# Opening of a hybrid decoder block on one core: modulation and state-space products by channel halves, transfers issued from the SyncE queue

## What is computed

```
c_act = silu(c)
mod = c_act @ w_ada + b_ada                  # six rows of 1024: sh1, sc1, g1, sh2, sc2, g2
h = rmsnorm(x, norm1_g) * (1.0 + sc1) + sh1
z = h @ w_in                                 # 1024 x 3584: conv input and gate, ssm input, two gates
u_conv, u_ssm, gl_conv, gl_ssm = split(z)
y_conv = conformer_conv(u_conv, ...)         # 31-tap causal depthwise convolution, layernorm, silu, projection
y_ssm = s5_mixer(u_ssm, ...)                 # 32 groups of 16 channels, 64 complex states, gelu, GLU
merged = sigmoid(gl_conv) * y_conv + sigmoid(gl_ssm) * y_ssm
x = x + g1 * (merged @ w_out)
```

## Time and profile before

| | us |
|---|---|
| median of 3 runs | 2529.43 |
| lowest, highest | 2527.99, 2530.13 |
| the profiled execution | 2530.5 |
| its span | 2528.7 |
| PE busy in the span | 2489.5 |
| DVE, ACT, POOL busy | 1651.0, 875.9, 1724.7 |
| mean granted TensorE clock, share of full | 0.994 |

### The profile page before, as it was taken

One profiled execution on the slowest core, in us unless ns is written; L12 is line 12 of the kernel. 1 busy time (PEld: TensorE's weight loads), 2 busy tenths in 40 slices (PEclk: granted clock), 3 DMA queues, 4 the chain that ended last, 5 costly groups with the idle time before them and its releaser, 6 DMA issues.

```text
span 2528.7 us, 31370 instructions
## 1 busy us (share of the span) xinstructions
PE 2489.5 (98%) x11419; PEld 2050.1 (81%) x11419; DVE 1651.0 (65%) x2038; ACT 875.9 (35%) x1379; POOL 1724.7 (68%) x1182
## 2 busy tenths in 40 slices
PE   7999999999999999999999999999999999999998
PEld 3888788888888888888788888878878888888886
DVE  5899639945596648946833334575654336899798
ACT  4322421153012421146533345443222334445444
POOL 2777777677866777675787767797778764445444
PEclk9999999999999999999999999999999999999999
DMA  8676357553666347472332232324566327465533
GB/s 278 201 200 217 117 161 222 155 167 119 212 173 191 123 159 224 136 225 90 123 96 76 79 112 93 109 86 148 175 190 193 103 88 252 144 226 183 197 99 117
DMA packets 426161, 395.66 MB, mean 156 GB/s; under 512 B 92232, under 2 KB 330520, under 8 KB 424472
## 3 DMA queue, kind: packets, MB, share of 16 engines
q1 hardware_dynamic: 324688, 319.93, 40.6%
q10 hardware_dynamic: 101320, 73.72, 9.5%
HBM read 317.88 MB, written 67.24 MB: 152 GB/s over the span
## 4 chain that ended last, share of the span: by engine, by line
PE 84%; DVE 6%; DMA 3%; issue 2%; ACT 2%; POOL 1%; ACTq 1%; SPq 0%; POOLq 0%; DVEq 0%
PE bank L1926 19%; PE bank L1928 19%; PE bank L1927 19%; PE bank L2171 5%; PE bank L2172 5%; PE bank L2173 5%; DMA row_pair<-in_w_ffn_out 3%; PE bank L2085 2%; PE bank L2087 2%; PE bank L2086 2%; PE bank L2006 1%; PE bank L2005 1%; DVE bank L1027 1%; PE bank L1991 1%; DMA ada<-in_w_ada 1%
## 5 line engine op out<-in xcount | busy, mean ns | idle before, releaser
L2258 POOL TENSOR_TENSOR w_lo<-raw,w_hi 128x1024 fp32r<-128x1024 f32 x192 | 479.6, 2498 | 36.7 <-ACT w_hi L1383 12.5
L2254 POOL CAST w_hi<-raw 128x1024 fp32r<-128x1024 f32 x186 | 199.5, 1073 | 346.2 <-PE bank L1928 272.0
L1926 PE MATMUL bank<-h_hi,w_hi 128*128 128x512 f32 x896 | 352.3, 393 | 1.0 <-ACT wm L1322 0.9
L1928 PE MATMUL bank<-h_hi,w_lo 128*128 128x512 f32 x896 | 349.9, 390 | 0.0
L1927 PE MATMUL bank<-h_lo,w_hi 128*128 128x512 f32 x896 | 349.5, 390 | 0.0
L839 DVE SCALAR_TENSOR_TENSOR bank<-uc,cwt,bank 128x512 f32<-128x512 f32 x464 | 323.2, 751 | 6.2
L2281 POOL TENSOR_TENSOR fw_lo<-fsum,fw_hi 128x512 fp32r<-128x512 f32 x176 | 237.8, 1355 | 71.3 <-ACT fw_hi L1615 71.2
L1926 PE MATMUL bank<-xc_hi_T,fw_hi 128*128 128x512 f32 x704 | 276.4, 393 | 5.8 <-DVE tr L1032 4.6
L1927 PE MATMUL bank<-xc_lo_T,fw_hi 128*128 128x512 f32 x704 | 274.8, 390 | 0.0
L1928 PE MATMUL bank<-xc_hi_T,fw_lo 128*128 128x512 f32 x704 | 274.6, 390 | 0.0
L2308 POOL TENSOR_TENSOR ow_lo<-raw,ow_hi 128x512 fp32r<-128x512 f32 x116 | 161.4, 1392 | 163.3 <-ACT ow_hi L1662 163.3
(11 more groups left out here) (341 smaller groups left out, 5246.4 us busy)
## 6 DMA issues: line engine op xcount, KB each, us to landing
raw<-in_w_in SPq DMA_DIRECT2D x112, 512.0 KB, 3.9
raw<-in_w_ffn_in SPq DMA_DIRECT2D x66, 512.0 KB, 6.0
hid_scratch<-tr SPq DMA_DIRECT2D x88, 256.0 KB, 3.2
raw<-tsum_scratch SPq DMA_DIRECT2D x66, 256.0 KB, 3.2
g2b<-in_w_ada SPq DMA_DIRECT2D x64, 256.0 KB, 3.9
ssm_m<-vk_scratch SPq DMA_DIRECT2D x32, 512.0 KB, 5.0
raw<-in_ssm_glu SPq DMA_DIRECT2D x32, 512.0 KB, 3.8
raw<-in_w_out SPq DMA_DIRECT2D x32, 512.0 KB, 3.6
```

Of the source, the lines that this page charges most:

```text
L1926: t.matmul(dst, wh, xh, start=first, stop=False)
L1928: return t.matmul(dst, wl, xh, start=False, stop=last)
L2254: g.tensor_copy(hi[:], src[:]).then_inc(hi_done, 1)
L2258: g.tensor_tensor(lo[:], src[:], hi[:].bitcast(F32), ALU.subtract).then_inc(split_done, 1)
```

## The change

The change rewrites the opening of block 0.

- **Halves.** The modulation is made in two halves by output channel (kinds sh1 and sc1 together). PE's rows of half 0 go into `bank[2]`, of half 1 into `bank[7]`. Each half has its own sums, `modrow`, turn and scale (`modulation_sums`, `modulation_turn` and `modulation_half`). PE keeps slabs 1, 3 and 5; DVE takes 0, 2, 4, 6 and 7.
- **Products.** The first four weight chunks are no longer one per output tile. Chunk (pair, half) holds 256 output columns, which are two ssm tiles, for 4 of the 8 channel tiles. PE runs pair 0 on channels 0 to 3 (step "A0"), then pair 1 on 0 to 3 ("A1"), then pair 0 on 4 to 7 and pair 1 on 4 to 7 (`ssm_rest`). us0 and us1 are thus done together, and so are us2 and us3.
- **Order.** PE puts the turns, the sums of the second half, the transposes of h4 to h7 and those of `nat_b` between these products; `nat_w` (v2) comes after hl7 and ahead of the products of channel tile 7. DVE puts the first angles and the mean and root of x's norm ahead of slab 2, and slab 4's four steps between hl0 and hl3. ACT applies h0 to h3 ahead of the exponentials and sines.
- **Transfers.** c comes by itself in `nat_c`, issued first by ACT, and is turned on PE into `bank[6]`, from where ACT takes silu; a Silu on one column ("pre") goes ahead of it. ACT issues that, two tiles of x and the step sizes. SP issues the rest: slab 0, two tiles of x, slab 1, the vectors, the poles, slabs 2 and 3, two weight chunks, slabs 4 to 7, `nat_b`, the next two chunks, and then the small parameters.

The diff, cut to its core:

```diff
-    FIRST_CHUNKS = [ssm_chunks + sum(conv_chunks, [])]
+    FIRST_CHUNKS = [[("us", pair_, half) for half in range(2) for pair_ in range(KS // 2)] + sum(conv_chunks, [])]
...
-        pe_pro = ["v1", "ada1", "v0", "ada3", "ada5", "ada6", "ada7", "sums", "mt"] + h_steps[0:4] + ["bx"] + h_steps[4:] + ["v2"]
+        pe_pro = ["vc", "ada1", "v1", "v0", "ada3", "sums0", "h0", "h1", "mt0", "h2", "h3", "A0", "ada5", "h4", "sums1",
+                  "mt1", "h5", "bx", "A1", "h6", "h7", "v2"]
...
-        act_pro = ["cs", "dt"] + norm_act + [f"nx{i}" for i in R(TT)] + ["ej", "m8", "sj", "cj"] + h_act
+        act_pro = ["pre", "cs", "dt"] + norm_act + [f"nx{i}" for i in R(TT)] + h_act[:2 * KH] + ["ej", "m8", "sj", "cj"]
+        act_pro += h_act[2 * KH:]
...
+            def modulation_half(half):
+                dve.wait_ge(*tensor.after("pro", f"sums{half}"))
+                link(v.tensor_copy(modrow[half][:], mod_bank[half][0:2, :]), f"modrow{half}")
+                dve.wait_ge(*tensor.after("pro", f"mt{half}"))
...
             slab_sum(0)
-            slab_sum(2)
-            norm_mean("pro")
-            slab_sum(4)
-            norm_root("pro")
+            dve.wait_ge(*tensor.after("pro", "v1"))
+            for cols in (slice(0, 6 * KD), slice(7 * KD, nv_rows)):
+                link(v.tensor_copy(vt[:, cols], bank[7][:, cols]), "vt")
             dve.wait_ge(*tensor.after("pro", "v0"))
...
+            norm_mean("pro")
...
+            norm_root("pro")
+            slab_sum(2)
             angles(jarg[:, 0, :, :], jarg[:, 1, :, :], jtmp[:], th, T + 1, "jargs")
...
+            modulation_half(0)
+            for k in R(KH):
+                h_split("pro", k)
+                slab_step(4, k)
+            slab_sum(6)
+            slab_sum(7)
...
+            modulation_half(1)
...
+            def ssm_products(pair_, k):
+                pe.wait_ge(*vec.after("pro", f"hl{k}"))
+                hi, lo = (w[pair_][:].rearrange("p (k n) -> p k n", n=2 * P) for w in (w_hi, w_lo))
+                for j in R(2):
+                    m, cols = 2 * pair_ + j, slice(j * P, (j + 1) * P)
+                    ins = three(bank[plan[0, f"us{m}"]][:], hi[:, k % KH, cols], lo[:, k % KH, cols],
+                                h_hi[:, k, :], h_lo[:, k, :], k == 0, k == KD - 1)
+                    if k == KD - 1:
+                        ins.then_inc(*tensor.step(0, f"us{m}"))
+                return ins
...
+            transposes("pro", 0)
+            transposes("pro", 1)
+            modulation_turn(0)
+            pe.wait_ge(*scal.after("pro", "cs"))
+            transposes("pro", 2)
+            pe.wait_ge(split_done, RAW + 1)
+            transposes("pro", 3)
+            for k in R(KH):
+                ins = ssm_products(0, k)
+            ins.then_inc(*tensor.step("pro", "A0"))
+            pe.wait_ge(pro_v, mark["vt"])
+            modulation_rows(5)
+            pe.wait_ge(pro_v, mark["scale00"])
+            pe.wait_ge(pro_v, mark["poles"])
+            transposes("pro", 4)
+            modulation_sums(1, [(0, "slab6", 1), (1, "slab7", 0)])
+            pe.wait_ge(split_done, RAW + 2)
+            ssm_products(1, 0)
+            modulation_turn(1)
+            ssm_products(1, 1)
+            pe.wait_ge(pro_v, mark["scale01"])
+            transposes("pro", 5)
+            parameter_rows()
+            ssm_products(1, 2)
+            ssm_products(1, 3).then_inc(*tensor.step("pro", "A1"))
...
+            load_slab(0)
+            for i in R(2, TT):
+                sp.dma_start(xs[:, i, :], x_d[i * P:(i + 1) * P, :]).then_inc(xs_in, 16)
+            load_slab(1)
```

More of the change, by code:

```diff
@@ L653, in scale_of, with slab_step @@
                                      ALU.mult), f"scale{which}")
-            dve.wait_ge(*tensor.after("pro", "v1"))
-            link(v.tensor_copy(vt[:], bank[1][:, 0:nv_rows]), "vt")
             dve.wait_ge(*scal.after("pro", "cs"))
             link(v.tensor_copy(zc[:, :, 3], cact), "zc")
+            def slab_step(n, j):
+                kind, half, rows = SLABS[n]
+                part = (half + kind) % 2
+                sums = acc[:, part * HALF:(part + 1) * HALF]
+                k = rows * KD // 2 + j
+                if j == 0:
+                    dve.wait_ge(ada_in[n % ADA], 16 * (n // ADA + 1))
+                if k == 0 or n == 7 and j == 0:
+                    link(v.tensor_scalar(sums, ada[n % ADA][:, j, :], cact[:, k:k + 1], None, ALU.mult))
+                else:
+                    link(v.scalar_tensor_tensor(out=sums, in0=ada[n % ADA][:, j, :], scalar=cact[:, k:k + 1],
+                                                in1=sums, op0=ALU.mult, op1=ALU.add),
+                         f"slab{n}" if j == KD // 2 - 1 else None)
@@ L660, in slab_sum @@
             def slab_sum(n):
[L661 to L663 removed]
                 for j in R(KD // 2):
[L665 to L671 removed]
+                    slab_step(n, j)
@@ L1853, in modulation_rows, with modulation_sums, modulation_turn @@
                 ins.then_inc(*tensor.step("pro", f"ada{n}"))
+            def modulation_sums(half, parts):
+                for kind, slab, part in parts:
+                    pe.wait_ge(pro_v, mark[slab])
+                    ins = t.matmul(mod_bank[half][0:2, :], one_row[:, 3 - kind:5 - kind],
+                                   acc[:, part * HALF:(part + 1) * HALF], start=False, stop=slab == parts[-1][1])
+                ins.then_inc(*tensor.step("pro", f"sums{half}"))
+            def modulation_turn(half):
+                pe.wait_ge(pro_v, mark[f"modrow{half}"])
+                for j in R(4):
+                    ins = t.transpose(mod_bank[half][:, 2 * j:2 * j + 2], modrow[half][:, j * P:(j + 1) * P],
+                                      ident[0:2, 0:2])
+                ins.then_inc(*tensor.step("pro", f"mt{half}"))
@@ L1861, in _ @@
-            for r, name in enumerate(("slab2", "slab4")):
-                pe.wait_ge(pro_v, mark[name])
-                ins = t.matmul(bank[7][0:4, :], one_row[:, 3 - r:7 - r], acc[:, r * HALF:(r + 1) * HALF], start=False,
-                               stop=r == 1)
-            ins.then_inc(*tensor.step("pro", "sums"))
-            pe.wait_ge(pro_v, mark["modrow"])
-            for j in R(4):
-                ins = t.transpose(bank[7][:, 4 * j:4 * j + 4], modrow[:, j * P:(j + 1) * P], ident[0:4, 0:4])
@@ L1894, in _, with three @@
-            for k in R(4, KD):
-                transposes("pro", k)
-            pe.wait_ge(taps_in, 16 * KC)
-            pe.wait_ge(pro_v, mark["scale0"])
-            turn_rows_in(2, nat_w, bank[7])
+            def three(dst, wh, wl, xh, xl, first, last):
+                t.matmul(dst, wh, xh, start=first, stop=False)
+                t.matmul(dst, wh, xl, start=False, stop=False)
+                return t.matmul(dst, wl, xh, start=False, stop=last)
+            def ssm_products(pair_, k):
[8 more added lines that the diff above has]
+                return ins
@@ new lines, in parameter_rows @@
+            def parameter_rows():
+                pe.wait_ge(bx_in, 64)
+                pe.wait_ge(*vec.after("pro", "hl3"))
+                for n in R(2):
+                    turned = bank[4 + n][:].rearrange("p (g h) -> p g h", h=HG)
+                    for h in R(HG):
+                        ins = t.transpose(turned[:, :, h], nat_b[n][:, :, :, h].rearrange("g a p -> g (a p)"),
+                                          ident[0:G, 0:G])
+                ins.then_inc(*tensor.step("pro", "bx"))
@@ new lines, in ssm_rest @@
+            def ssm_rest():
+                pe.wait_ge(split_done, RAW + 3)
+                for k in R(KH, KD):
+                    if k == KD - 1:
+                        pe.wait_ge(taps_in, 16 * KC)
+                        pe.wait_ge(*vec.after("pro", "hl7"))
+                        turn_rows_in(2, nat_w, bank[7])
+                    ssm_products(0, k)
+                    if k < KH + 2:
+                        transposes("pro", k + 2)
+                pe.wait_ge(split_done, RAW + 4)
+                for k in R(KH, KD):
+                    ssm_products(1, k)
@@ L1922, in kernel_tiles @@
                     ins.then_inc(*tensor.step(0, f"kk{n}"))
[L1924 to L1928 removed]
             def mixers(b, last=False):
[L1931 removed]
+                chunk = [0 if b else KS]
                 def next_chunk():
@@ L2313, in _, with load_slab @@
         def _(sp):
-            for n, (kind, half, rows) in enumerate(SLABS):
+            def load_slab(n):
+                kind, half, rows = SLABS[n]
                 col = kind * D + half * HALF
```

167 lines of the change are left out of this document (80 added, 87 removed).

## The result

The change makes the kernel slower: 2544.97 us (median of 4 runs, 2544.20 to 2545.58) against 2528.71 of the kernel before on the same chip; ratio 1.0061, interval 1.0049 to 1.0073 (the ratios here are those of the measurement, over all fast runs of both kernels, and not quotients of the two medians). The forecast was 2530.0 and the range ended at 2536. The profiled span is 2542.4 us, 13.7 more than before.

What follows compares the result with a forecast made beforehand. PE was taken as the bound, busy 2489.5 of 2528.7 us. Profiled 2530.5 - 0.25 (state matrix earlier) + 0.8 (clock) = 2531.05, so the median goes from 2529.4 to 2530.0 us; range 2526.0 to 2536.0.

Steps and rivals of the forecast that it cites:

- Part 3: From us0 to the state matrix: PE's 5.8 us gain ends in two waits, for DVE and ACT; ua1 0.25 us earlier.
- ACT has no slack there: At the state matrix: ACT's `wm` copies, behind a table load at 84.21 and 32 DMA issues, hold PE 0.91 us.
- Part 4: PE's clock: 0.8 us charged once to us0's end, range 0 to 3; nothing charged for the state matrix.
- Parts 1 and 2: The opening: hl3 ends at 36.3, A0 near 38, second half's sums until 44.0, us0 done at 61.4.
- PE's four matmuls on it cost half of 6.55 us, 3.3 us: Opening, slab 1 on PE: 3.3 us from landing at 13.5, then 0.5 for the turn; DVE has `vt` at 17.4.
- The same instructions, plus ... 17.4 + 10.3 = 27.7.: DVE's first half: earlier 5.25 us stretch plus small instructions (2.0) and slab 2 (3.11), from 17.4 to 27.7.
- slabs 6 and 7, 3.11 each: DVE's second half: slab 4's last step, then both slabs, taking it from 36.3 to 43.4.
- Slab 5 on PE, 1.7, ... hidden: PE behind A0: slab 5 takes 1.7 us, hidden behind DVE's work; PE waits from about 40.5.
- The clock rival: Interleaved stretch: PE at lower clock for six to eight us, twice with the state matrix; 2536; chance 13%, finally 0.10.
- the rival of late vectors: SP's queue: slab 1 or vectors behind slab 3, DVE 5 to 6 us later; 2535.5; chance 0.04 for late data.
- same: Whole kernel: the change moves waits and no end, with us0 done anywhere from 59.5 to 66; chance 0.80.

Runs made afterwards that it cites:

- vectors_first: Changed kernel with vectors and poles issued by SP ahead of slab 1 and turned on PE ahead of its slab 1 matmuls; 2540.15 us, ratio 1.0048.
- bx_split: Changed kernel with the 32 `nat_b` transposes in two halves, before and after the products of channel tile 2 of pair 1; 2542.54 us, ratio 1.0059.
- before_turns_late: Kernel before, with ACT issuing the 16 small loads of ssm tiles 2 and 3 after the state matrix; 2533.2 us, ratio 1.0018.
- before_turns_by_sp: Kernel before, with the small loads of ssm tiles 2 and 3 issued by SP instead of ACT; 2526.71 us, ratio 0.9989.
- pool_held: Changed kernel with POOL's first split of a weight chunk held until DVE's angles are done; 2543.64 us, ratio 1.0057.
- slab7_on_pe: Changed kernel with slab 7 moved back from DVE to PE, behind A0; 2548.63 us, ratio 1.0078.
- slabs57_before_h: Changed kernel with slab 7 back on PE and slabs 5 and 7 multiplied there ahead of the first sums; 2544.84 us, ratio 1.0069.
- after_turns_late: Changed kernel, with ACT issuing the 16 small loads of ssm tiles 2 and 3 after the state matrix; 2546.33 us, ratio 1.0073.
- before_slab6_on_dve: Kernel before, with slab 6 moved from PE to DVE, behind the angles; 2533.53 us, ratio 1.0014.
- after_six: Changed kernel: vectors and poles first, POOL's first split held, slabs 5 and 7 on PE ahead of h3, `nat_b` in two halves; 2540.82 us, ratio 1.0054.
- after_six_turns_by_sp: after_six plus seven DVE parameter instructions ahead of hl6 and the small loads of ssm tiles 2 and 3 issued by SP; 2537.28 us, ratio 1.0034.

## Why the prediction was wrong

**The tail was right in its mechanism.** Prediction, Part 3: PE's earlier end goes into a wait of 3.3 us for `cwt` and one for ACT (seen 3.42, then 1.34 and 0.90); from `uz` to the table load 21.8 or 23.3 us (seen 23.25, with a slow eight at 4.69). PE was to reach the state matrix 16.9 us behind us0 (78.3 less 61.4), and did so 17.0 us behind `uz`. The forecast set the shift at 4.45 us less than the lateness of `uz` (+4.2 gives -0.25). The ten kernels that keep ACT's order show 2.0 to 4.9 less; vectors_first and bx_split 4.5, the change itself 2.4. Its missing 2.1 are about what the clock took: `cx` at the lower level, 1.97 instead of 1.03 us, and 10 us instead of 7 from 151 on, between ua1 (+15.4) and 165 us (+16.8) another 1.4. So one term of the tail was mis-sized: Part 4 charged nothing for the clock at the state matrix. In nine of the ten kernels where PE waited 3.4 us for `cwt`, the clock fell there; in the six without such a wait the same 40 transposes stayed at 1.00, as Part 4's row at 88 did. And "ACT has no slack there" was too strong (before_turns_late, before_turns_by_sp): in the kernel before PE's own work ends last, and ACT costs it some 0.3 us. ACT becomes a bound only when `uz` is late or PE early.

**The steps that failed are in Parts 1 and 2: `uz` at 61.4 was forecast, 76.4 came.** In order:

1. *"PE's four matmuls on it cost half of 6.55 us, 3.3 us"*. The row has x8 because a float32 matmul leaves two records. 32 records in 16.75 us are four slabs of four, and 6.55 us is one slab, for the most part at the lower clock; at the full clock it is 3.60. (The windows print 1.00 at 12 to 14 us, but the records of the granted clock begin only at 18.03, and at 21.46 in the change. The matmul records are 0.85 us apart in this slab, as they are between 22.5 and 27 at 0.50, and 0.43 apart at 1.00.) **+3.25 us**, a misread row. Counting the instructions in the order of the program (x4 per slab) beside the trace's x8 would have shown it.
2. Slab 1 came at 15.4, not 13.5, **+1.85**. The rate dipped to 198 GB/s from 10 to 12 us and 318 from 12 to 14, from about 416 before. What slowed it no run separates. Items 1 and 2 are 5.0 us at `vt` (22.35 against 17.4; the terms add up to 5.1).
3. *"The same instructions, plus ... 17.4 + 10.3 = 27.7."* They were costed without POOL, whose two splits had been beside an idle DVE before and now stood beside them: **+4.9** at `modrow` (shown by pool_held: 5.1). The order of POOL was never laid beside DVE's.
4. *"slabs 6 and 7, 3.11 each"* and *"Slab 5 on PE, 1.7, ... hidden"*. Slab 7 took 5.4 us beside POOL's third split, +2.3 on DVE. On PE A0 ended at 49.5, not 1.7 but 3.7 us behind hl3, its first seven products at the lower clock, and slab 5 took 3.6: both engines reach the second sums within 0.5 us. From `modrow` of the first half to that of the second it took 18.7 us, where 16.3 were forecast: **+2.4**. That both engines are on the path is in part argued: slab7_on_pe shows that moving slab 7 behind A0 on PE costs 2.9 us, and slabs57_before_h moves the second `modrow` 2.2 us forward though the first is 2.7 later.
5. The clock, charged 0.8: the stretch behind `nat_b` was at 0.50 for over 6 us, twelve products took 5.3 us instead of 2.7, **+2.6**. From the second `modrow` to `uz` it took 20.05 us, where 17.4 were forecast; after_turns_late, with the same order of PE and without the fall, took 17.49.

5.0, 4.9, 2.4 and 2.6 are 14.9 of the 15.0 us. The clock rival (13%) had the mechanism of item 5, but asked for T0 (us0 done) past 66.5 from the clock alone; the rival of late vectors had the right place, DVE starting 5 us late, with another cause, and gave 2535.5. Neither was added to the other, and items 1 and 3 were in no case at all. The chance of 0.80 for "same" rested on a T0 with a slack of 5 us; each of the first two sums of errors, 5.0 and 4.9, used it up alone.

What the prediction named as signs against itself came: the lower clock for more than 4 us between 40 and 67, and ua1 off by more than 3 us.

**What stays open.** Why the feed-forward layer takes up to 3.5 us more or less from kernel to kernel (for the change it is the clock at two places; before_slab6_on_dve loses 3.0 us between 1700 and 2000 us with no more of the lower clock there than before); what makes the clock fall in the interleaved stretch (after_six and after_six_turns_by_sp have the same order of PE there and were low for 3.5 and 14 us; the change and after_turns_late for 7 and for none); how an early opening could avoid the low stretch near 140 us.

## What to carry to other kernels

Work that is moved forward lands beside other work: lay every engine's new timeline over the moved stretch, also that of an engine which the change doesn't touch (here POOL), before pricing it with durations taken from a quiet stretch. Check what one record of a group is against the program's order before dividing its time. When a time depends on a date, add the errors of all the terms that lead to the date, and compare their sum with the slack, not each alone.
